# A residual block with a sparse-attention indexer: two stages' orders of work planned with other costs, the end of a search cut into jobs, rows and minima kept differently

## The reference

```python
rel = jax.nn.relu(jnp.einsum('bqhd,bkd->bqhk', q_idx, k_idx))          # 16 indexing heads
score = jnp.einsum('bqh,bqhk->bqk', w_idx, rel)                         # one score for each key
top_val, top_idx = lax.top_k(score, 256)                                # the 256 best keys
# group B: 8 heads attend to these keys alone, one key/value head, distance bias (ALiBi)
# group A: 4 heads over all keys, two softmax maps each:
attn = softmax(s1 * scale + bias) - lam * softmax(s2 * scale + bias)
o = rmsnorm(attn @ v, subln_g) * (1 - lam_init)
```

## Time and profile before

| | us |
|---|---|
| median of 3 runs (lowest, highest) | 3531.5 (3530.02, 3533.46) |
| span of the profiled execution | 3528.7 |
| first projection, to | 294.3 |
| indexing, to | 1035.2 |
| values, to | 1075.9 |
| attention, to | 2034.4 |
| output projection and MLP, to the end | 3528.7 |

### The profile page before, as it was taken

One profiled execution on the slowest core, in us unless ns is written; L12 is line 12 of the kernel. 1 busy time (PEld: TensorE's weight loads), 2 busy tenths in 40 slices (PEclk: granted clock), 3 DMA queues, 4 the chain that ended last, 5 costly groups with the idle time before them and its releaser, 6 DMA issues. The chain is left out here.

```text
span 3528.7 us, 44735 instructions
## 1 busy us (share of the span) xinstructions
PE 3215.3 (91%) x15808; PEld 2589.9 (73%) x15808; DVE 2505.4 (71%) x4762; ACT 1860.6 (53%) x3101; POOL 427.3 (12%) x690
## 2 busy tenths in 40 slices
PE   5998988988987889989889989999989999999998
PEld 4787767876755666767667778778878878888787
DVE  6444788888875676777868667878788775665676
ACT  4313777877766778878787633432242223222232
POOL 0011122101200000000000000022112120000231
PEclk9999999999985999989999999999999999999999
DMA  6575433323336432211211236354444445664555
GB/s 226 165 234 139 116 104 101 89 69 99 108 123 160 109 93 50 49 47 41 54 25 37 73 127 216 129 190 141 157 162 150 154 175 195 244 224 167 195 214 199
DMA packets 330637, 471.76 MB, mean 134 GB/s; under 512 B 25328, under 2 KB 217024, under 8 KB 330032
## 3 DMA queue, kind: packets, MB, share of 16 engines
q1 hardware_dynamic: 280576, 305.09, 28.8%
q0 software_dynamic: 49840, 163.83, 13.7%
HBM read 311.84 MB, written 156.98 MB: 133 GB/s over the span
## 5 line engine op out<-in xcount | busy, mean ns | idle before, releaser
L2363 PE MATMUL m_ps<-m_h,w_hi 128*128 128x512 f32 x1792 | 558.1, 393 | 19.5 <-DVE w_lo L1965 10.3
L2363 PEld LDWEIGHTS m_ps<-m_h,w_hi 128*128 128x128 f32 x1792 | 337.8, 189 | 95.4 <-DVE w_lo L1965 15.9
L921 PE MATMUL isps<-ki,iq 128*128 128x512 f32 (+3 forms) x1216 | 308.1, 389 | 69.5 <-ACT spare L951 51.8
L1029 DVE SCALAR_TENSOR_TENSOR rank<-spare,iw,rank 128x1024 f32<-128x1024 f32 (+5 forms) x330 | 329.8, 1021 | 58.1 <-ACT spare L951 53.9
L2376 PE MATMUL m_ps<-w_hi,a_hi 128*128 128x512 f32 x896 | 350.1, 391 | 6.3 <-DVE w_lo L2194 3.4
L2363 PE MATMUL m_ps<-m_h,w_lo 128*128 128x512 f32 x896 | 350.9, 392 | 0.0
L2376 PE MATMUL m_ps<-w_lo,a_hi 128*128 128x512 f32 x896 | 349.9, 390 | 0.0
L2376 PE MATMUL m_ps<-w_hi,a_lo 128*128 128x512 f32 x896 | 349.7, 390 | 0.0
L921 PEld LDWEIGHTS isps<-ki,iq 128*128 128x128 f32 x1216 | 231.2, 198 | 144.7 <-issue 39.2
L951 ACT ACTIVATE spare<-isps 128x1024 f32<-128x1024 f32 (+5 forms) x352 | 276.7, 818 | 65.8 <-PE isps L921 51.5
L2861 PE MATMUL tps<-ident,probs 128*128 128x128 f32 x1632 | 240.4, 290 | 58.2 <-DVE probs L3077 54.7
(11 more groups left out here) (294 smaller groups left out, 6646.0 us busy)
## 6 DMA issues: line engine op xcount, KB each, us to landing
w_raw<-in_w_ff SPq DMA_DIRECT2D x136, 512.0 KB, 5.4
dram_aop<-a_out POOLq DMA_DIRECT2D x224, 256.0 KB, 2.6
a_lo<-dram_aop SPq DMA_DIRECT2D x56, 1024.0 KB, 5.4
queries<-dram_proj SPq DMA_DIRECT2D x128, 256.0 KB, 4.3
iq<-dram_proj SPq DMA_DIRECT2D x224, 128.0 KB, 3.0
ada_w<-in_w_ada POOLq DMA_DIRECT2D x16, 1024.0 KB, 6.6
dram_proj<-r_ev_hi POOLq DMA_DIRECT2D x104, 128.0 KB, 2.7
dram_proj<-r_ev_lo POOLq DMA_DIRECT2D x104, 128.0 KB, 2.8
```

Source lines behind the costliest of these rows:

```text
L921: mm = nc.tensor.matmul(sps[:, job.n % 2, a:b], iq[:, job.unit % IQU, job.head % 2, part, :], ki[:, job.c * SCH + a:job.c * SCH + b], star ...
L1029: nc.vector.scalar_tensor_tensor(out=dst, in0=got, scalar=w, in1=dst, op0=ALU.mult, op1=ALU.add).then_inc(s_acc, 1)
L2363: mm = nc.tensor.matmul(ps[:, b], w[:, w1_slot(n, j), k, :], hop[:, j, h, :, k, :], start=fresh and k == 0 and i == 0, stop=k == KH - 1 an ...
```

## The change

- **Planner's costs.** Every job has, beside its cost, a time `late` after which its result can be seen, and every engine a time before it sees one. Transfers (stores of products, masks, weights, mixed outputs, masks asked for) become jobs of a stream each, with a time to land; what overwrites their buffer waits for the landing in the plan. PE's jobs take twice their cost while the plan holds PE's clock to be halved, which it follows from how busy it has planned PE. All offsets, keys and places of the searches are other numbers.
- **Searches.** The start is cut in two (maximum, then steps), the mask into five jobs. The table of step sizes is one multiplication of a constant row of powers of two.
- **Indexing** has three query buffers instead of two, and `tie` and `below` are shorter.
- **Attention** has a second row `second_odd` for the second map of every other dense head, one row `bias` instead of two, three places of 128 columns in `mixst` with two semaphores instead of one place of 256 used by all. SP asks for the mask of the next block at the end of a block's loads instead of at their start.
- **Maxima.** The instruction that reads scores multiplies by minus the slope and keeps the minimum; a second piece starts from the minimum of the first. So it yields what the exponential takes as its bias; only the first map of a dense head adds a shift. A dense head inverts its two sums in one instruction.

The diff, cut to its core:

```diff
+                after = [(read[n - 2], 0.0)] if n >= 2 else []
+                if unit not in last_of_unit and unit >= IQU:
+                    after.append((last_of_unit[unit - IQU], 3.1))
...
-        freed.append(put(chain, Step("mask", "DVE", 1.2 + 6.6 * size, k + 1 + ROUNDS, [last], block=b, k=k)))
+        for part, cost in enumerate((0.47 + 1.045 * size, 0.19 + 1.045 * size, 0.19 + 2.085 * size,
+                                     0.25 + 1.045 * size, 0.09 + 1.045 * size)):
+            after = [(last, 0.0)] + ([(freed[k - 1], 0.0)] if part == 1 and k else [])
+            last = put(chain, Step("mask", "DVE", cost, 0.08, k + 1 + ROUNDS + INDEX_MASK, after, part=part, **more))
...
+            stores.append(put("store", Step("store", "Q", 0.55 if full else 2.15, 2.4, where, [(ends[m], 0.0)], tile=tile,
+                                            g=g, n=m)))
...
-                        then(nc.vector.tensor_scalar(steps[:, q, 0:1], col(TK_R), -1.0, None, ALU.mult))
-                        at = 1
-                        while at < TOPK_ROUNDS:
...
+                        nc.vector.tensor_scalar(steps[:, q, :], powers[:], col(TK_R), None, ALU.mult).then_inc(s_thr[q], 1)
...
-            masks[i] = add("bias", Job("bias", "DVE", 0.2 + 1.07 * size, 6 * i - 1.0, None,
-                                       [reads[i - 2]] + ([kept[i]] if i in kept else []), block=i, length=length))
+            after = [reads[i - 1]]
+            if i in kept:
+                after.append(add("chosen", Job("chosen", "Q", 0.6, 3.5, 6 * i - 1.0, None, [kept[i], masks[i - 1]], **more)))
+            masks[i] = add("bias", Job("bias", "DVE", 0.053 + 1.043 * size, 0.083, 6 * i - 1.0, None, after, **more))
...
-        bias = sb("bias", [P, 2, SEQ])
+        bias = sb("bias", [P, SEQ])
+        second_odd = sb("second_odd", [P, SEQ])
...
-        mixst = sb("mixst", [P, 2 * P])
+        mixst = sb("mixst", [P, 3 * P])
...
-                    nc.scalar.activation(row, row, ACT.Exp, bias=stat[:, job.hm % 8, 2:3], scale=slope,
+                    row = row_of(job)[:, 0:job.length]
+                    nc.scalar.activation(row, row, ACT.Exp, bias=stat[:, job.hm % 8, 2:3], scale=-1.0,
...
+                    to = 2 if job.last else 0
-                                                   in0=sps[:, job.score.n % 2, 0:job.width], in1=add, scale=1.0,
-                                                   scalar=-3e38, op0=ALU.add, op1=ALU.max,
-                                                   accum_out=st[:, job.c:job.c + 1]).then_inc(s_sf, 1)
-                    if job.last:
+                                                   in0=sps[:, job.score.n % 2, 0:job.width], in1=add, scale=-slope,
+                                                   scalar=st[:, 0:1] if job.c else 3e38, op0=ALU.add, op1=ALU.min,
+                                                   accum_out=st[:, to:to + 1]).then_inc(s_sf, 1)
+                    if job.last and job.what == "map1":
                         dve.wait_ge(s_sf, job.read)
-                        if job.chunks == 2:
-                            then(nc.vector.tensor_tensor(st[:, 0:1], st[:, 0:1], st[:, 1:2], ALU.max))
-                        shift = SHIFT_EXP if job.what == "map1" else 0.0
-                        nc.vector.tensor_scalar(st[:, 2:3], st[:, 0:1], -slope, shift, ALU.mult,
-                                                ALU.add).then_inc(s_negm, 1)
+                        nc.vector.tensor_scalar(st[:, 2:3], st[:, 2:3], SHIFT_EXP, None, ALU.add).then_inc(s_negm, 1)
```

## The result

The changed kernel takes 3330.3 us (median; 3329.18 to 3334.68), the kernel before beside it 3531.3: a ratio of 0.9433, 95% interval 0.9418 to 0.9448. That is 201 us less, where 108 were forecast and 3365 was the lowest time in the range. The direction was right, the size was not.

The account below looks back on a forecast made before the run. Order and waits, with no engine full, were taken to bound indexing and attention; terms of 55 us and 53 us, 108 together, off 3531.5 gave 3423.5, stated as 3423 us, range 3365 to 3505.

Parts of the forecast that it names:

- term f: In attention: running minima drop small DVE instructions, so exponentials start sooner after their scores; 12 us (0 to 32).
- The rival 'slower': In attention: searches fall behind at 10 us a round instead of 8.7, giving 3567 us; chance 0.07.
- the half clock: In attention: TensorE's granted clock stays about 0.93, as transposes before attention ran at 0.50; no gain counted.
- all waits and the half clock go: Rival for both stages: indexing at 650 us, attention at 849, whole time 3331; chance 0.06.
- i (second row): In attention: a second row for map 2 cuts TensorE's waits for combined rows; 12 us (0 to 40).
- h (places): In attention: three places for mixed outputs instead of one cut ACT's waits on a store; 8 us (0 to 18).
- g (masks): In attention: the four masks in pieces give back half of ACT's loss around them; 16 us (0 to 32).
- c (landings): In indexing: stores planned with a landing time, so ACT's waits for them are spent otherwise; 10 us (0 to 35).
- a: In indexing: each search's mask cut into five jobs lets sums in between; 30 us (0 to 52).
- b: In indexing: a third query buffer cuts PE's waits for query loads; 8 us (0 to 16).
- j and k: In attention: own queue place for mask loads, 8 us (-10 to 12); one bias row, -3 us (0 to -20).
- ACT at 82.5%, as in its better third: In attention: at 905 us the whole stage would go at ACT's pace from 1590 to 1925 us.

Follow-up runs that it names:

- f4: The kernel before, with indexing's masks in pieces and attention's running minima added, its old planner and offsets kept: 3535.5 us.
- e3: The changed kernel with attention's old maxima and two query buffers in indexing instead of three, offsets kept: 3369.3 us.
- e7: The changed kernel with the transposes that make the values written as matmuls with the identity: 3335.9 us.
- i1: The changed kernel with masks in one job, two query buffers, one second row and one place for mixed outputs, offsets fitted anew: 3414.1 us.
- i4: The changed kernel with all parts, but old durations, one hand-over of 0.15 us, no landings, no halved clock in the planner, offsets fitted anew: 3482.6 us.
- e2: The changed kernel with each search's mask as one planner job again in indexing and attention, offsets kept: 3414.4 us.
- g2: The changed kernel with the old offsets, keys and slacks of the streams in both stages, new costs kept: 3428.3 us.
- the control: The changed kernel with only the planner's slack moved by 2 to 3 per cent in each stage: 3382.2 us.
- j1 to j5: Changed kernel, offsets refitted, with attention's masks whole; one second row; one output place; full-clock planning; no landings planned: 3336.1, 3359.2, 3345.2, 3333.8, 3369.2 us.

## Why the prediction was wrong

**What held.** The stages, the waits and their order were the right ones, and the MLP didn't move. The last mask of indexing ended at 865.8 us (947 before), PE's ReLU wait fell under 25 us, no gap of PE over 5 us at a mask is left, 64 instructions of 154 ns are left (L3174), and term f measured 8 to 12 us for 12 (f4, e3). The rival 'slower' did not come: attention's four searches took 745 us instead of 833, 7.8 us a round, and the last mask ended at 1747 us (1913 before). Of the other signs, ScalarE's wait for stores is 8 us and not near 0, and attention still dips at masks (ACT 15.38 of 20 us from 1213.5, where 8.37 stood). The new form of the read, whose start value comes from memory, was bounded by 20.4 us. It costs 62 ns for 1024 scores (the same difference at 896 to 512), and 128 reads have it, 8 us of DVE (an estimate from these); the multiplication by the slope costs nothing (1221 ns, 1223 before):

```profile
L3168 DVE CUSTOM_DVE_ANT_0 probs<-sps,bias 128x1024 f32<-128x1024 f32 x72 | 87.8, 1221 | 48.1 <-PE sps L2941 34.3 <-PE tps L2957 13.5
...
L3168 DVE CUSTOM_DVE_ANT_0 probs<-sps,bias,stat 128x1024 f32<-128x1024 f32 x8 | 10.3, 1283 | 1.0 <-PE sps L2941 0.2
```

**What failed first: the half clock, "I count none of it".** 42 of attention's 112 us are PE's busy time, up to 36 of them by the clock, and the sign that was named against the forecast, a clock of 0.97 in attention, came: 0.98. (These 42 us are part of what the parts and the planner measure below, and don't come on top.) The argument rested on one row, the values at 0.50, taken as the sign for all of attention's transposes. e7 shows that the row was read rightly for the stretch it comes from, 64 transposes with 32 small products: 0.50, and 1.00 once the transposes were matmuls. The step that failed is carrying it over to attention: there 1632 of PE's 5344 instructions are transposes, with scores and products between them, and in steps of 20 us the clock is at 1.00 from 40 us after the start, but for one dip (0.92, then 0.99, from 1093.5 to 1133.5). The transposes themselves take 278 ns each from then on, where those of the values take 432. The rows for its second, third and fourth 20 us:

```profile
1013.50:1033.50 20.00, 18.73 (x84) 14.58 (x82) 9.99 (x48) 15.17 (x47) 2.69 (x5) 0.63 0.67 151
1033.50:1053.50 20.00, 15.98 (x99) 11.34 (x100) 13.12 (x53) 17.98 (x53) 3.23 (x6) 1.00 0.69 162
1053.50:1073.50 20.00, 16.39 (x99) 11.30 (x98) 14.54 (x49) 18.79 (x52) 2.15 (x4) 1.00 0.67 162
```

The trace of before had contradicted the argument: 0.98 from 1590 to 1925, with 632 of the same transposes in it (L2861), 279 ns each. A row from another stage was preferred to one from the stage in question. The clock of indexing had no term either, and no reason was given for that; 24 us of PE's busy time went there. The rival "all waits and the half clock go" (3331 us, 0.06) came nearest, with 846 us in attention where it said 849 and 657 in indexing where it said 650, though not all waits went.

**What failed second: sizes of terms, from shares of a wait.** The two of attention that reach the short blocks were too small: i (second row) 29 for 12, h (places) 15 to 20 for 8; g (masks) was too large, 6 for 16. i and h were a quarter and a half of a wait summed over the stage, but the loss sits in blocks 0 to 7. There lay 31.8 of the 54.7 us that PE waited for combined rows before the change, and 16.9 of ACT's 18.5 for stores of mixed outputs. Why a stop costs more there than its own length isn't shown. In indexing c (landings) was 34 for 10, at the upper end of its bounds (35); a and b, 38 together, were 16. The stage as a whole, 84 us, stayed inside its ends of 20 and 90; attention's 112 did not (10 and 90).

**What failed third: a term that was not there.** In attention I priced parts alone. The new durations and hand-overs had no term, though they were the first point of the change. Parts measured 63 us (i1) and minima 12; the other 37 us are the planner's, the fit's, or belong to j and k, which I didn't isolate. Taken the other way round, the old costs alone lose 98 (i4), so there is no one share for either. "ACT at 82.5%, as in its better third" was taken for a limit on that; ACT now runs at 737 of 846, 87%.

**A sign that came true by luck.** In indexing, terms a and b were to gain 38 us by letting sums in, and PE's ReLU wait did fall. But at block 10's mask no sum came in; projection work lay beside it. And without the cuts the wait falls as well: to 24.3 us in e2 and 12.6 in i1, where the one long stop, 10.1 us, is at block 10's mask.

**Left open.** What the new precedence of streams is worth by itself: g2 lost 61 us in indexing and 33 in attention, and the second is less than the control's 43. How much of i4's 98 us is durations and how much hand-overs. The 12 us of indexing that neither i1's parts nor i4's costs account for, if the two add up. And how good each new fit is: a loss of i1, i4 or j1 to j5 holds, beside the part, whatever the random steps missed.

## What to carry to other kernels

Where a planner's offsets have been fitted, first move one of them by a few per cent and run that: what it loses is the size under which a kernel with one part undone says little, and parts should be compared with the offsets fitted anew. A wait that comes from a plan that lacks a landing can be worth most of its length: in indexing 34 us for a wait of 46.5 that fell to 8.1, though in attention nothing. For TensorE's clock, read the rows of the stage in question: here less idle time of PE (49 us for 119 in attention, 14 for 74 in indexing) came together with a higher granted clock (0.98 for 0.93, 0.99 for 0.96), and with 42 and 24 us less of PE's busy time for the same instructions.

## What the runs showed of the hardware

In the making of the values, 64 transposes and 32 small products, TensorE was granted 0.50 of full clock though busy for 5.00 of 5 us (changed kernel, 965 to 975 us); with these transposes written as matmuls with the identity it was granted 0.77 in the first of the same two steps and 1.00 in the second (e7). In attention, with 1632 transposes among 5344 instructions, it was granted 0.98, and 1600 of these transposes, from 40 us after the start on, took 278 ns each, where the 64 of the values took 432. The 64 float32 transposes of the values, written as matmuls, ran as 128 instructions (e7, L1223, 306 ns each). A read of 1024 scores from PSUM that keeps a running minimum took 1283 ns when its start value came from memory and 1221 without, 62 ns more (changed kernel, L3168).
